# A mixture-of-experts stage: weight rows grouped eight to a partition, tokens gathered as whole rows to 64 partitions

## What is computed

```python
def hier_moe(h, lw):
    t = h.reshape(-1, D_MODEL)                                  # 640 x 1024
    p_g, g_idx = lax.top_k(softmax(t @ lw['w_grp']), 1)         # 4 groups
    ...
    top_w, top_i = lax.top_k(p_e, 2)                            # 2 of the group's 8 experts
    top_w = p_g * top_w / jnp.sum(top_w, axis=-1, keepdims=True)
    combine = ...                                               # 640 x 32, two entries a token
    a = jnp.einsum('td,edf->tef', t, lw['w_up'])                # w_up, w_gate: 32 x 1024 x 256
    g = jnp.einsum('td,edf->tef', t, lw['w_gate'])
    act = jax.nn.silu(g) * a * combine[:, :, None]
    return jnp.einsum('tef,efd->td', act, lw['w_down'])         # w_down: 32 x 256 x 1024
```

## Time and profile before

| | us |
|---|---|
| median of 3 runs | 1115.89 (1114.41 to 1116.38) |
| the profiled execution | 1117.27, of which its span is 1115.3 |
| PE busy in the span | 916.1 (82%) |
| DVE, ACT, POOL busy | 388.7, 265.1, 137.9 |
| mean rate of DMA | 191 GB/s over the span |
| expert stage, from the first gather to the last scatter | about 748 to 1077 |

### The profile page before, as it was taken

The page is one execution under the profiler, slowest core; times in us unless marked ns, Lnnn a source line. Parts: engine busy times, 40 slices in busy tenths (PEclk is TensorE's granted clock), DMA queues, the critical chain, the costliest instruction groups (busy, mean ns, idle before and its releaser), DMA issues.

```text
span 1115.3 us, 14394 instructions
## 1 busy us (share of the span) xinstructions
PE 916.1 (82%) x5822; PEld 702.9 (63%) x5822; DVE 388.7 (35%) x758; ACT 265.1 (24%) x449; POOL 137.9 (12%) x182
## 2 busy tenths in 40 slices
PE   3669898988999999999999796729988888876640
PEld 3467544447999999999999685625544444443320
DVE  1544534461525252522244533461211111111028
ACT  4337534351121212121122311302111111111003
POOL 0000000000000000000000300312333323232233
PEclk9789999898999999999999898958989999998785
DMA  8601366420222222211123085556999999997863
GB/s 304 224 6 39 114 231 245 147 76 1 76 75 75 75 75 75 75 57 58 57 62 118 29 256 127 190 215 253 414 415 416 417 416 415 412 372 297 336 238 150
DMA packets 87707, 212.86 MB, mean 191 GB/s; under 512 B 11488, under 2 KB 43704, under 8 KB 87016
## 3 DMA queue, kind: packets, MB, share of 16 engines
q1 hardware_dynamic: 81160, 201.03, 49.0%
q0 software_dynamic: 6496, 11.12, 2.7%
HBM read 206.26 MB, written 15.81 MB: 199 GB/s over the span
## 4 chain that ended last, share of the span: by engine, by line
PE 60%; DMA 19%; DVE 8%; SPq 4%; ACT 3%; issue 2%; POOL 2%; POOLq 0%; DVEq 0%; ACTq 0%
DMA w_ug<-in_w_gate 13%; PE pair L952 11%; PE pair L954 11%; PE pair L956 11%; PE pair L589 6%; PE pair L1088 3%; PE pair L1109 3%; DMA xg<-h_rows,at_g 2%; SPq L386 2%; PE pair L945 2%; PE pair L971 2%; PE pair L946 2%; PE pair L947 2%; PE pair L608 2%; PE pair L1100 2%
## 5 line engine op out<-in xcount | busy, mean ns | idle before, releaser
L589 PE MATMUL pair<-w_ug,xgT 128*64 128x256 f32 x1216 | 160.2, 423 | 50.3 <-DMA w_ug<-in_w_gate 49.1
L589 PEld LDWEIGHTS pair<-w_ug,xgT 128*64 128x64 f32 x1216 | 94.4, 152 | 103.4 <-issue 36.2
L952 PE MATMUL pair<-hT,hi 128*128 128x320 f32 x640 | 145.9, 309 | 2.2 <-DVEq L1560 2.2
L954 PE MATMUL pair<-hT,hi 128*128 128x320 f32 x640 | 145.9, 309 | 0.0
L956 PE MATMUL pair<-hT,lo 128*128 128x320 f32 x640 | 145.7, 309 | 0.0
L1412 DVE TENSOR_TENSOR lo<-raw,hi 128x2048 fp32r<-128x2048 f32 (+3 forms) x36 | 80.1, 2224 | 162.3 <-ACT hi L1245 161.6
L1245 ACT CAST hi<-raw 128x2048 fp32r<-128x2048 f32 (+3 forms) x36 | 66.7, 1853 | 254.1 <-PE pair L956 207.2
L952 PEld LDWEIGHTS pair<-hT,hi 128*128 128x128 f32 x640 | 106.9, 188 | 2.4 <-DVEq L1560 2.4
L956 PEld LDWEIGHTS pair<-hT,lo 128*128 128x128 f32 x640 | 107.1, 188 | 0.0
L954 PEld LDWEIGHTS pair<-hT,hi 128*128 128x128 f32 x640 | 107.0, 188 | 0.0
L797 DVE TENSOR_TENSOR act_v<-pair,sa 64x256 f32<-64x256 f32 x38 | 15.8, 417 | 203.9 <-ACT sa L656 203.9
(11 more groups left out here) (246 smaller groups left out, 1200.4 us busy)
## 6 DMA issues: line engine op xcount, KB each, us to landing
w_ug<-in_w_up SPq DMA_DIRECT2D x38, 1024.0 KB, 16.7
w_ug<-in_w_gate SPq DMA_DIRECT2D x38, 1024.0 KB, 19.4
w_dn<-in_w_down SPq DMA_DIRECT2D x38, 1024.0 KB, 19.4
raw<-in_w_in SPq DMA_DIRECT2D x20, 1024.0 KB, 5.2
ada_b<-in_w_ada SPq DMA_DIRECT2D x16, 1024.0 KB, 6.1
ada_a<-in_w_ada SPq DMA_DIRECT2D x8, 1024.0 KB, 12.1
ya<-expert_rows SPq DMA_DIRECT2D x5, 1024.0 KB, 6.9
raw<-in_w_conv_out SPq DMA_DIRECT2D x4, 1024.0 KB, 5.1
```

Of the source, the lines that this page charges most:

```text
L589: x = pe.matmul(bank[2 + d % 2][g * SL:(g + 1) * SL, 0:DE], xgT[d % 2][:, k, h * SL:(h + 1) * SL], w_ug[r][:, g, h, k, :], start=(n == 0), ...
L952: pe.matmul(o, st[0], m[0], start=first, stop=False)
L954: pe.matmul(o, st[0], m[1], start=False, stop=False)
```

## The change

The expert weights w_up and w_gate are now cut as `(p k)`: a partition holds eight neighbouring rows, 8 KB in one piece in DRAM and in SBUF. The gather takes 64 indices and reads whole rows of H2D (4 KB) to partitions 0 to 63, so `xg` is 64 x 1024. The turn takes eight slices of 64 x 128, with a column step of eight, each to 64 columns of the bank; the bank and the copy behind it keep their size. In the up-projection the loop over halves is gone, with the same 16 instructions. The gather's list is now the token itself, and the lists take two instructions. The wait for the gather in the turn is taken by itself, which in the loop adds one semaphore increment on PE.

```diff
@@ -195,8 +195,8 @@
     p6.close()
     p6_bytes = sum(placed[p6_first:])
     placed.clear()
-    xg = [sb(f"xg{i}", [P, HD]) for i in range(2)]
-    xgT = [sb(f"xgT{i}", [P, 4, P]) for i in range(2)]
+    xg = [sb(f"xg{i}", [SL, D]) for i in range(2)]
+    xgT = [sb(f"xgT{i}", [P, KD, SL]) for i in range(2)]
     yo = [sb(f"yo{i}", [P, HD]) for i in range(2)]
     sa = [sb(f"sa{i}", [SL, DE]) for i in range(2)]
     act_v = [sb(f"act_v{i}", [SL, DE]) for i in range(2)]
@@ -218,7 +218,7 @@
     r_ev = sb("r_ev", [P, X_MAX // 2])
     val = sb("val", [P, 2, NT, 3])
     gate2 = sb("gate2", [P, 2, D])
-    ug_late = [sb(f"w_ug{i}", [P, 2, 2, 4, DE]) for i in range(2, RING)]
+    ug_late = [sb(f"w_ug{i}", [P, 2, KD, DE]) for i in range(2, RING)]
     dn_late = sb("w_dn2", [P, 2, D])
     spare = sb("spare", [P, (RINGS - sum(placed) + 31) // 32 * 8])
     assert sum(placed) >= RINGS
@@ -227,7 +227,7 @@
     gate1 = sb("gate1", [P, 2, D])
     sq2 = sb("sq2", [P, D])
     p7 = ExitStack()
-    w_ug = [sb(f"w_ug{i}", [P, 2, 2, 4, DE], scope=p7) for i in range(2)] + ug_late
+    w_ug = [sb(f"w_ug{i}", [P, 2, KD, DE], scope=p7) for i in range(2)] + ug_late
     early = ExitStack()
     h2T = sb("h2T", [P, KD, T], scope=early)
     early.close()
@@ -383,7 +383,7 @@
                 sp.wait_ge(s_ug, nth(j0, d - RING))
             e = expert_of(j0, d)
             for n, w in enumerate((io["w_up"], io["w_gate"])):
-                sp.dma_start(w_ug[r][:, n], w[0][bass.ds(e, 1)].rearrange("a (h p k) c -> p (a h) k c", h=2, p=P)
+                sp.dma_start(w_ug[r][:, n], w[0][bass.ds(e, 1)].rearrange("a (p k) c -> p (a k) c", p=P)
                              ).then_inc(ug_in[r], 16)
 
         def load_down(j0, d):
@@ -464,16 +464,15 @@
             pool.tensor_copy(t[d % 2][:, :], lists[:, which, bass.ds(j0 + d, 1)]).then_inc(s_at, 1)
             wait_alone(pool, s_at, nth(j0, d))
 
-        h2_half = H2D.rearrange("t (h c) -> (t h) c", h=2)
         y_half = YD.rearrange("t (h c) -> (t h) c", h=2)
 
         def gather(j0, d):
             p = d % 2
             index(at_g, 0, s_atg, j0, d)
             pool.indirect_dma_start(
-                out=xg[p][:, :], out_offset=None, in_=h2_half,
-                in_offset=bass.IndirectOffsetOnAxis(ap=at_g[p][:, :], axis=0),
-                bounds_check=2 * T - 1, oob_is_err=False).then_inc(gat[p], 16)
+                out=xg[p][:, :], out_offset=None, in_=H2D,
+                in_offset=bass.IndirectOffsetOnAxis(ap=at_g[p][0:SL, :], axis=0),
+                bounds_check=T - 1, oob_is_err=False).then_inc(gat[p], 16)
 
         def scatter(j0, d):
             p = d % 2
@@ -571,10 +570,10 @@
         x.then_inc(s_lists, 1)
 
         def turn(j0, d):
-            pe.wait_ge(gat[d % 2], nth_dma(j0, d))
-            cols = xg[d % 2][:, :].rearrange("p (q k) -> p k q", k=4)
-            for k in range(4):
-                x = pe.transpose(bank[d % 2][:, k * P:(k + 1) * P], cols[:, k, :], ident)
+            wait_alone(pe, gat[d % 2], nth_dma(j0, d))
+            cols = xg[d % 2][:, :].rearrange("s (p k) -> s k p", k=KD)
+            for k in range(KD):
+                x = pe.transpose(bank[d % 2][:, k * SL:(k + 1) * SL], cols[:, k, :], ident[0:SL, 0:SL])
             x.then_inc(s_tr, 1)
 
         def up(j0, d):
@@ -583,11 +582,10 @@
             pe.wait_ge(s_xgT, nth(j0, d))
             if not (isinstance(j0, int) and d < 2):
                 pe.wait_ge(s_act, nth(j0, d - 2))
-            for n in range(8):
-                h, k = n // 4, n % 4
+            for k in range(KD):
                 for g in range(2):
-                    x = pe.matmul(bank[2 + d % 2][g * SL:(g + 1) * SL, 0:DE], xgT[d % 2][:, k, h * SL:(h + 1) * SL],
-                                  w_ug[r][:, g, h, k, :], start=(n == 0), stop=(n == 7))
+                    x = pe.matmul(bank[2 + d % 2][g * SL:(g + 1) * SL, 0:DE], xgT[d % 2][:, k, :],
+                                  w_ug[r][:, g, k, :], start=(k == 0), stop=(k == KD - 1))
             x.then_inc(s_ug, 1)
 
         def act_turn(j0, d):
@@ -647,7 +645,7 @@
 
         def xg_out(j0, d):
             act.wait_ge(s_tr, nth(j0, d))
-            act.copy(xgT[d % 2][:, :, :], v3(bank[d % 2], 4, P)).then_inc(s_xgT, 1)
+            act.copy(xgT[d % 2][:, :, :], v3(bank[d % 2], KD, SL)).then_inc(s_xgT, 1)
 
         def silu(j0, d):
             act.wait_ge(s_ug, nth(j0, d))
@@ -776,7 +774,8 @@
                           ALU.is_equal).then_inc(s_hots, 1)
 
         dve.wait_ge(s_lists, 1)
-        dve.tensor_scalar(lists[:, :, :], v3(bank[7], 2, TILES), 2.0, cst[:, K_HALF:K_HALF + 1], ALU.mult, ALU.add)
+        dve.tensor_scalar(lists[:, 0, :], bank[7][:, 0:TILES], float(FAR), None, ALU.add)
+        dve.tensor_scalar(lists[:, 1, :], bank[7][:, TILES:2 * TILES], 2.0, cst[:, K_HALF:K_HALF + 1], ALU.mult, ALU.add)
         dve.tensor_copy(weights[:, :], bank[7][:, 2 * TILES:3 * TILES]).then_inc(s_rdy, 1)
 
 
```

## The result

The changed kernel takes 1128.31 us (median of 6 runs, 1126.76 to 1133.33) against 1115.15 us for the kernel before (6 runs). The ratio of the two is put at 1.0144, with a 95% interval of 1.0118 to 1.0171: 16 us slower. It isn't the quotient of the two medians, which lie 13.2 us apart, at the lower end of the interval. The forecast was 7.5 us slower, and 1123.4 us; the range to 1130 holds the time, but by the ratio the loss is double what was forecast.

The account below looks back on a forecast made before the run. DMA engines serving the low slots were taken to bound the expert stage; packets -4.5, gather +10.6, loop +1.3 and start 0 gave +7.4, rounded +7.5 us, so 1123.4 us, range 1109.5 to 1130.

Parts of the forecast that it names:

- What bounds the kernel: Expert stage, tiles 4 to 31: 28 tiles run at the pace of the DMA engines that serve the low slots.
- The packets: Up and gate weights: one 8 KB packet costs 310 ns, two of 4 KB 322; 0.16 us a tile, -4.5 us.
- the loop: Last six tiles, three rounds with a ring of two: +0.42 us a round, +1.3 us in all.
- The gather: Token rows in 28 tiles: partitions 0 to 63 get double the gather bytes, +0.38 us a tile, +10.6 us.
- The turn: Transposes of gathered tokens on PE: eight take 0.95 us, +0.2 us, hidden in the DMA-bound stretch, on the path in loop rounds.
- the start: Head of the expert stage: lists +0.2 us, fewer descriptors 0 to 0.7 back, first turn +0.2; sum 0, within +-0.7.
- The cover of the gather's latency: Gather packets alternating with longer weight packets: +0.6 us on a 6.3 us median, hidden by over 8 us a step.
- The signs: 8 KB packets at 310 ns, count down a third, at most 415 GB/s, share below 1.03, gate wait about 57 us, longer tail.
- the even spread: Rival: the gather spreads evenly over all 16 engines, so no doubling, -4.5 us stands alone: 1111.5 us; chance 0.24.
- four neighbouring rows on each engine: Rival: 16 engines move four rows each; the gather's added 0.16 us a tile cancels the packets' saving: 1116.5 us; chance 0.15.
- packets that stay at 4 KB: Rival: weight transfers still cut into 4 KB: 1128.3 us with the slower gather, 1116.0 with an even one; chance 0.04 each.
- PE as the bound: Rival: the turn grows beyond the 1.4 us of PE idle time a tile; +8 us, 1120.4 us; chance 0.06.

Follow-up runs that it names:

- the weights alone: Kernel before with up and gate weights loaded as eight neighbouring rows a partition, gather and turn as before: 1110.24 us, ratio 0.9976.
- the gather alone: Not run by itself: ratio 1.0161 of changed gather and turn less 1.0017 of the changed turn, against the kernel before: 0.0144, 16.0 us.
- the even deal: Tokens of a tile dealt evenly over the slots by another constant: in the kernel before 1109.32 us, ratio 0.9967; in the changed kernel 1130.36 us, 1.0153.
- The turn alone: Kernel before with a turn of eight slices of 64 partitions, only the first 64 partitions of the gathered rows turned: 1115.17 us, ratio 1.0017.
- gather and turn alone: Changed kernel with up and gate weights loaded as in the kernel before, two 4 KB pieces a partition: 1130.46 us, ratio 1.0161.
- The run with rows at both ends and the even deal: Changed kernel, 128 indices, rows gathered to partitions 0 to 31 and 96 to 127, eight 128 x 128 transposes, tokens dealt evenly over slots: 1112.64 us, ratio 1.0007.
- the run with the matrix of ones: Changed kernel with even slots on partitions 0 to 63, odd on 64 to 127, turned by multiplying with a 128 x 64 matrix of ones: 1210.64 us, ratio 1.0876.

## Why the prediction was right or wrong

**What bounds the kernel.** Right. The stretch runs at the pace of the DMA engines, and of those that serve the low slots: dealing the slots evenly gained 3.7 us and brought the engines from some 12 us apart to 5.

**The packets.** -4.5 us in the stretch and -0.5 in the loop; the weights alone gave -2.7 (interval -4.7 to -0.7). Right in sign, and the price of a packet was right: 38.5 us a MB over a mix of two thirds 8 KB packets, where 310 and 161 ns give (2 x 37.8 + 39.3) / 3 = 38.3. The time fell short of it by nearly half. In the profiled execution all of the gain, 3.2 us, is in the stretch and none in the loop; that is what 420 GB/s against 415 are worth over 250 us, and two thirds of the 4.5 counted by the packet.

**The gather: the step that failed.** The mechanism was the right one, the destination and not the packets, and the price of the rows doubled, as was said: 14.8 us became 30. What was mis-sized is the price to be doubled. I took 0.38 us a tile for 28 tiles, 10.6 us, and 1.1 in the loop, 11.7 together; the gather alone cost 16.0 us, and the rows of the kernel before, taken away, gave 14.8. In the stretch the rows of the kernel before are worth 251.9 - 237.5 = 14.4 us, 0.51 a tile, and those of the changed kernel 266.9 - 236.9 = 30.0, so the doubling added 15.6, 0.56 a tile. The 0.38 was chosen near the mean of 16 engines (0.35), though the same paragraph held that the engines of the fullest slots set the pace, with 0.64 as their bound. The traces bear that paragraph out, since the engines drift some 12 us apart over the stage. A value half way, 0.50 x 28 = 13.9 us, would have been near; it is picked with the result in view, but the side on which 0.38 would err could be read ahead. The loop isn't where the forecast failed: it was priced at 1.3 us, with 3.3 as its bound, and lost 2.8 in the profiled execution.
Nor was the way it costs quite as I saw it. I expected half the engines to run dry, with a share below 1.03. The share is 1.02, so none runs dry to speak of, and the weights' packets grew from 161 to 167 ns in the mean with their sizes unchanged. That fits rows moved by engines of both halves that meet at one half's way in; it is inferred from the durations, since the profile doesn't tell one engine from another, and the 64 indices in place of 128 stand beside it as a cause that no run took away alone. The rule of the Trainium skill ("SBUF — State Buffer", "Door 1: The DMA port swizzle") that partitions 0 to 63 reach 8 ports of 16 agrees with the doubled price: rows to one half cost 30 us, and back on both ends of the partitions the loss is gone. It doesn't tell why the even deal did nothing with the rows in one half. Its measured ratio of 1.67 for one transfer alone gave an estimate of +6.6 us where the runs have +16.0; its count of ports, twice, was the better guide.

**The turn.** +0.2 us forecast. The timeline of one tile, which answers to the earlier trace rows (start us, us):

```profile
903.51 1.09 PE L576 MATMUL pair<-cst,xg 64*128 64x64 f32 x8
...
909.09 3.24 PE L587 MATMUL pair<-w_ug,xgT 128*64 128x256 f32 x28 [2.35 <-DMA w_ug<-in_w_gate]
```

The turn takes 1.09 us against 0.75, longer by 0.34 and not 0.2, within the bound of 0.6; before the next up PE still waits 2.35 us for its weights. The turn alone cost 1.9 us (interval 0.2 to 3.6), where 0.6 had been counted in the loop and 0.2 at the start. That it hides in the stretch fits: PE still waited 52.0 us for gate weights.

**The cover of the gather's latency.** Right in the stretch, not at the head. A longer wait of 0.6 us was expected to hide. From 820 to 983 us it did: a gather lands after 6.9 us, and PE waits 1.2 us in all for rows. At the head of the stage it lands 2 us later (8.3 us in the median from 770 to 830 us, against 6.3), and the step through gather and scatter grew from some 6.5 to 7.4 us and more, near the 8.6 us that a tile takes in the stretch; over the whole stage PE waited 11.8 us for rows, against 7.5. Neither half of the change does this alone: from 770 to 830 us the median is 6.9 us with the weights alone and 6.9 with gather and turn alone. What these waits cost was not separated. The run with rows at both ends and the even deal waits even 16.4 us for rows and is within some 3 us of the kernel before.

**The sum.** The experiments give -2.7 + 17.9 = 15.2 for the weights and for gather and turn, against 16 measured, where the forecast had 7.5. Of the 7.7 us between, 4.3 are the gather, 2.3 the packets and 1.1 the turn. The start cost nothing: the first gather reached its turn in 3.5 us against 3.4.

**The signs.** The packets' count fell by a third and the rate below 415 GB/s, as said. The tail is longer, too: the parts of the last unrolled loads land 14.1 to 16.1 us apart, against 11.6 to 12.7. But PE's wait for gate weights went from 49.1 to 52.0 us only, where about 57 was given.

**The rivals.** The times of the even spread (1111.5 us) and of four neighbouring rows on each engine (1116.5) are refuted, and so are packets that stay at 4 KB. That the rows are moved by 16 engines is not refuted, and the stretched packets rather speak for it; what those two rivals had wrong is that only the engine counts, and not the half in which the rows land. PE as the bound didn't occur, but the run with the matrix of ones shows it: at 9.7 us a tile on PE, 3 us more a turn cost 97 us.

## What to carry to other kernels

Where DMA is the bound, a small transfer beside the big ones can cost more than its mean share of the engines (0.51 us a tile here, where the mean was 0.35), so ask which partitions its bytes land on and how full they are; gathering into half the partitions doubled the price of the rows from 15 to 30 us. Price a term at the engine that is last, not at the mean of 16, once the profile shows that they end apart. A list that fills from slot 0 can be dealt out over the partitions by a constant, at no cost, for 0.3%; with all rows going to one half it gave nothing. And cut a timeline where work is done, not where its loads are issued.

## What was not expected of the hardware

- The busy share of the DMA engines stays at 1.02 while the rate falls from 415 to 399 GB/s: here a full share is no sign of full speed, and the time for a MB (39.3, 40.3, 38.5 us) tells them apart.
- Eight float32 products with a slice of 128 x 128 as the stationary operand and 64 columns moving take 4.02 us (16 in the trace, 0.25 us each), where eight transposes of the same slices take 1.16 us, 0.14 each.
- Over 28 tiles the engines drift apart: the 16 parts of a 1 MB load land 0.7 us apart at tile 4 and some 12 at tile 31. Dealing the slots evenly brings this to 5, but not when 64 indices gather to one half (12.7 to 15.6).
- VectorE's scaling of 128 x 1024 elements went from 1.28 to 2.07 us, and GpSimd's addition from 2.35 to 2.85, with reads in steps of eight elements (the first block of each kernel).
